# End of the expert stage: last product and scatter by column halves, y ahead of the splits, overflow branch turned round

## What is computed

```python
xn = rmsnorm(h, norm_ffn[1])
h = h + moe_swiglu(xn, router, w_gate, w_up, w_down)     # 8 experts, top 2 of 8 for each token
gate = jax.nn.sigmoid(rmsnorm(h, ple_norm[1]) @ ple_gate[1])
h = h + gate * (p[1] @ ple_proj[1])                      # the "embedding" step
```

## Time and profile before

| | us |
|---|---|
| median of 3 runs | 2064.74 |
| lowest, highest | 2061.09, 2072.94 |
| the profiled execution, its own time | 2058.84 |
| its span from the first to the last instruction | 2057.0 |
| experts end, last product | 1521.06 |
| first gate product (0,0) starts | 1548.00 |

### The profile page before, as it was taken

How to read it: one execution, slowest core, us unless ns; L and a number is a source line. 1 busy time by engine, 2 the same in 40 slices (tenths; PEclk the granted TensorE clock), 3 DMA queues, 4 the chain that set the end, 5 groups by cost and what they waited for, 6 DMA issues and landing times.

```text
span 2057.0 us, 27400 instructions
## 1 busy us (share of the span) xinstructions
PE 1990.2 (97%) x10513; PEld 1680.8 (82%) x10513; DVE 1541.8 (75%) x1513; ACT 1243.8 (60%) x1346; POOL 0.2 (0%) x4
## 2 busy tenths in 40 slices
PE   8999999999899999999999999999979999999998
PEld 7879998887788888888888888888857787878786
DVE  4575556556788988988898898988877756766575
ACT  4554445555677777777777777776757444344532
POOL 0000000000000000000000000000000000000000
PEclk9999999999999999999999999999989999999999
DMA  8617555423799999999999999999974541344320
GB/s 262 215 41 254 187 188 165 155 82 121 254 376 345 357 370 338 374 334 367 341 354 379 326 374 346 358 376 326 375 270 130 179 144 62 123 164 164 123 82 21
DMA packets 243012, 504.08 MB, mean 245 GB/s; under 512 B 12136, under 2 KB 58984, under 8 KB 242920
## 3 DMA queue, kind: packets, MB, share of 16 engines
q1 hardware_dynamic: 242632, 502.71, 68.8%
q10 hardware_dynamic: 288, 0.11, 0.0%
HBM read 501.73 MB, written 1.05 MB: 244 GB/s over the span
## 4 chain that ended last, share of the span: by engine, by line
PE 84%; DVE 8%; ACT 4%; issue 2%; DMA 1%; SPq 1%; DVEq 0%; ACTq 0%
PE bank L693 25%; PE bank L695 25%; PE bank L694 25%; DVE low L1748 2%; PE bank L779 2%; PE bank L1123 1%; PE bank L1080 1%; PE bank L805 1%; ACT high L1299 1%; PE bank L664 1%; ACT high L1501 1%; PE bank L1208 1%; PE bank L796 1%; DMA raw<-in_w_in 1%; DVE y_lo L2361 1%
## 5 line engine op out<-in xcount | busy, mean ns | idle before, releaser
L2318 DVE TENSOR_TENSOR low<-raw,high 128x2048 fp32r<-128x2048 f32 x336 | 768.2, 2290 | 105.4 <-ACT high L1501 104.0
L1501 ACT ACTIVATE high<-raw 128x2048 fp32r<-128x2048 f32 x336 | 644.8, 1920 | 247.5 <-PE bank L695 246.2
L1748 DVE TENSOR_TENSOR low<-raw,high 128x2048 fp32r<-128x2048 f32 (+1 forms) x138 | 310.2, 2259 | 160.4 <-ACT high L1299 159.9
L1299 ACT ACTIVATE high<-raw 128x2048 fp32r<-128x2048 f32 (+1 forms) x138 | 260.7, 1894 | 165.0 <-PE bank L695 155.3
L693 PE MATMUL bank<-high,xg_hi 128*128 128x512 f32 x896 | 353.6, 395 | 2.2 <-DVE xg_lo L2301 2.2
L695 PE MATMUL bank<-high,xg_lo 128*128 128x512 f32 x896 | 349.4, 390 | 0.0
L694 PE MATMUL bank<-low,xg_hi 128*128 128x512 f32 x896 | 348.8, 389 | 0.0
L693 PE MATMUL bank<-high,xT_hi 128*128 128x512 f32 (+1 forms) x576 | 226.7, 394 | 4.1 <-DVE xT_lo L1764 1.8
L695 PE MATMUL bank<-high,xT_lo 128*128 128x512 f32 (+1 forms) x576 | 221.4, 384 | 0.0
L694 PE MATMUL bank<-low,xT_hi 128*128 128x512 f32 (+1 forms) x576 | 221.0, 384 | 0.0
L693 PE MATMUL bank<-high,hT_hi 128*128 128x512 f32 x536 | 210.1, 392 | 0.0
(11 more groups left out here) (315 smaller groups left out, 2366.1 us busy)
## 6 DMA issues: line engine op xcount, KB each, us to landing
raw<-in_moe_w_gate SPq DMA_DIRECT2D x112, 1024.0 KB, 5.5
raw<-in_moe_w_up SPq DMA_DIRECT2D x112, 1024.0 KB, 5.6
raw<-in_moe_w_down SPq DMA_DIRECT2D x112, 1024.0 KB, 5.7
raw<-in_w_in SPq DMA_DIRECT2D x63, 1024.0 KB, 5.4
raw<-in_w_out SPq DMA_DIRECT2D x20, 1024.0 KB, 4.9
raw<-in_dense_w_gate SPq DMA_DIRECT2D x11, 1024.0 KB, 5.3
raw<-in_dense_w_up SPq DMA_DIRECT2D x11, 1024.0 KB, 5.4
raw<-in_dense_w_down SPq DMA_DIRECT2D x11, 1024.0 KB, 5.0
```

The source lines that it names most:

```text
L1299: act.activation(high[:, slot, 0:k * n], raw[:, raw_slot[piece], 0:k * n], ACT.Copy).then_inc(high_done, 1)
L1501: act.activation(high[:, k % PARTS, :], raw[:, slot, :], ACT.Copy).then_inc(s["high"], 1)
L1748: dve.tensor_tensor(low[:, slot, 0:k * n], src, high[:, slot, 0:k * n].bitcast(F32), ALU.subtract).then_inc(low_done, 1)
L2318: dve.tensor_tensor(low[:, k % PARTS, :], raw[:, at0 + k % slots, :], high[:, k % PARTS, :].bitcast(F32), ALU.subtract).then_inc(s["low"], 1)
```

## The change

On all three engines the end of the last expert moves out of `expert` and `scatter` into a `finish`, and the beginning of the embedding step (`embedding_in`) moves into the branch. In the order of the code:

- **Down product.** The last half of the last expert's last down product runs column half 0 (bank 4) first, then column half 1; after the first a new semaphore `half` rises. The number of matmuls is the same.
- **y by halves.** ACT makes `y_hi` of half 0 behind `half`, that of half 1 behind the whole product. DVE raises `ylow` after each half. PE's scatter and DVE's adds go by columns first (n: token tile n % 2, columns n // 2).
- **Splits.** In the last expert only pp is split ahead (AHEAD = 1). pg0 half 0 is split behind y, at the start of `embedding_in(1)` (ACT: between y and the squares; DVE: between the last add and the norm); pg0 half 1 after the branch, by `splits(pp)`.
- **Branch.** `If(over < 1)` with the usual arm first: `finish` and `embedding_in(1)`, then `Else` with `finish`, the second pass, `finish` and `embedding_in(1)` again. The branch stands ahead of `finish`. PE reads the flag behind expert 0.
- **What is inside the usual arm.** PE: scatter, projection, transposes, gate product (0,0). ACT: root table, y, split of pg0 half 0, squares, root, the four takes of the projection, `xT_hi`. DVE: y, adds, split of pg0 half 0, 1/rms, rows, `xT_lo`.

```diff
+AHEAD = 1
@@ PE: product, in the last expert
-                            for f in range(2):
+                            columns_first = is_last and (j, half) == (GROUPS - 1, 1)
+                            for n in range(4):
+                                f, c = (n % 2, n // 2) if columns_first else (n // 2, n % 2)
...
+                                if columns_first and n == 1:
+                                    last.then_inc(s["half"], 1)
@@ PE
                 product("down", GROUPS - 1)
-                if is_last:
-                    scatter(e + 1, s, 12, turn_bank, range(4))
+            def finish(s):
+                for n in range(4):
+                    t, c = n % 2, n // 2
+                    cols = slice(c * CHUNK, (c + 1) * CHUNK)
+                    pe.wait_ge(s["ylow"], N_EXPERTS + c)
+                    pe.wait_ge(s["tfree"], 14 * N_EXPERTS - 5 + n)
+                    b = bank[6 + n % 2]
+                    pe.matmul(b[:, :], pickT[:, tok(t)], y_hi[:, cols], start=True, stop=False)
+                    pe.matmul(b[:, :], pickT[:, tok(t)], y_lo[:, cols], start=False, stop=True).then_inc(s["tfull"], 1)
@@ PE: all_experts
                 expert(0, s, first, True, False)
+                over = None
+                if not again:
+                    pe.wait_ge(route_ready, 1)
+                    over = pe.value_load(flag_i[0:1, 0:1], min_val=0, max_val=1)
                 with pe.Fori(1, N_EXPERTS - 1) as e:
@@ PE: experts
-                all_experts(moe_sems[0], moe_first, False)
-                pe.wait_ge(route_ready, 1)
-                over = pe.value_load(flag_i[0:1, 0:1], min_val=0, max_val=1)
-                with pe.If(over > 0):
+                over = all_experts(moe_sems[0], moe_first, False)
+                with pe.If(over < 1):
+                    finish(moe_sems[0])
+                    embedding_in(1)
+                with pe.Else():
+                    finish(moe_sems[0])
                     pe.wait_ge(moe_sems[0]["tfree"], 14 * N_EXPERTS)
                     pe.nop().then_inc(moe_sems[1]["used"], RAW)
                     all_experts(moe_sems[1], RAW, True)
-                    pe.wait_ge(redo_low, PARTS)
+                    finish(moe_sems[1])
+                    pe.wait_ge(redo_low, AHEAD)
+                    embedding_in(1)
@@ PE: embedding_in ends with
                 norm(("ple", l))
+                rows_half([("gate", l, 0, t) for t in range(NT)], ("pg", l, 0), 0, name=("ple", l))
@@ ACT: expert
-                    elif not again:
+                    elif not again and q + PARTS < PER_EXPERT + AHEAD:
                         split(moe_first + N_EXPERTS * PER_EXPERT + q + PARTS - PER_EXPERT)
...
+            def finish(s, first):
+                for c, (done, count) in enumerate(((s["half"], 1), (s["used"], first + PER_EXPERT * N_EXPERTS))):
+                    act.wait_ge(done, count)
+                    act.activation(y_hi[:, c * CHUNK:(c + 1) * CHUNK], bank[4 + c][:, :], ACT.Copy,
+                                   scale=slot_gate[:, 0:1]).then_inc(s["y"], 1)
+            def embedding_in(l, table=True):
+                if table:
+                    sqrt_ahead()
+                else:
+                    split_next()
+                half_squares(("ple", l), 0)
+                half_squares(("ple", l), 1)
+                serve_rstd()
+                for j in range(2):
+                    for t in range(NT):
+                        take(("pproj", l, j, t), projected(j, t))
+                norm_high(("ple", l))
@@ ACT: behind the experts
-                    with act.If(over > 0):
+                    with act.If(over < 1):
+                        sqrt_ahead()
+                        finish(moe_sems[0], moe_first)
+                        embedding_in(1, False)
...
+                    with act.Else():
+                        finish(moe_sems[0], moe_first)
...
@@ DVE: expert as ACT's, and
+            def finish(s):
+                for c in range(2):
+                    y_low(s, N_EXPERTS - 1, c).then_inc(s["ylow"], 1)
+                for n in range(4):
+                    t, c = n % 2, n // 2
                     cols = slice(c * CHUNK, (c + 1) * CHUNK)
+                    dve.wait_ge(s["tfull"], 14 * N_EXPERTS - 3 + n)
+                    dve.tensor_tensor(h[:, t, cols], h[:, t, cols], bank[6 + n % 2][:, :],
+                                      ALU.add).then_inc(s["tfree"], 1)
+            def embedding_in(l):
+                if l == 1:
+                    dve.wait_ge(moe_sems[0]["tfree"], 14 * N_EXPERTS)
+                    mark().then_inc(h_ready, 1)
+                    split_next()
+                norm_rows(("ple", l))
+                norm_low(("ple", l))
@@ DVE: experts
-                with dve.If(over > 0):
+                with dve.If(over < 1):
+                    finish(moe_sems[0])
+                    embedding_in(1)
...
+                with dve.Else():
+                    finish(moe_sems[0])
```

More of the change, by code:

```diff
@@ L263, in program @@
         members_ready, rank_max, route_ready = sem("members_ready"), sem("rank_max_ready"), sem("route_ready")
-        moe_names = ("sel", "tfull", "thigh", "tfree", "silu", "hm", "y", "ylow", "step")
+        moe_names = ("sel", "tfull", "thigh", "tfree", "silu", "hm", "half", "y", "ylow", "step")
         moe_sems = [{n: sem(f"moe{p}_{n}") for n in moe_names} for p in range(2)]
@@ L1192, in layer_embedding, with embedding_out @@
                 norm(("ple", l))
+                rows_half([("gate", l, 0, t) for t in range(NT)], ("pg", l, 0), 0, name=("ple", l))
+            def embedding_out(l):
                 for j in range(2):
                     for half in range(2):
-                        rows_half([("gate", l, j, t) for t in range(NT)], ("pg", l, j), half,
-                                  name=("ple", l) if j == 0 else None)
+                        if (j, half) != (0, 0):
+                            rows_half([("gate", l, j, t) for t in range(NT)], ("pg", l, j), half,
+                                      name=("ple", l) if j == 0 else None)
                         if (l, j, half) == (0, 1, 0):
@@ L1305, in splits, with split_next @@
                     split_no[0] += 1
+            def split_next():
+                split(split_no[0])
+                split_no[0] += 1
             def high_rows_of(key, dst, scales=None):
@@ L1642, in _ @@
                         act.wait_ge(moe_sems[1]["tfree"], 14 * N_EXPERTS)
-                    split_no[0] = moe_first + N_EXPERTS * PER_EXPERT + PARTS
-                norm_sums(("ple", l))
-                for j in range(2):
-                    for t in range(NT):
-                        take(("pproj", l, j, t), projected(j, t))
-                norm_high(("ple", l))
+                        sqrt_ahead()
+                        embedding_in(1, False)
+                if l == 0:
+                    embedding_in(0)
                 splits(pieces_of["pp", l][0])
@@ L2357, in expert, with y_low, embedding_in @@
                         gathered(s, 9 * e + 8, (7, 6))
+                if is_last:
+                    return
                 for c in range(2):
-                    cols = slice(c * CHUNK, (c + 1) * CHUNK)
-                    dve.wait_ge(s["y"], 2 * e + c + 1)
-                    last = dve.scalar_tensor_tensor(out=y_lo[:, cols], in0=bank[4 + c][:, :], scalar=slot_gate[:, 0:1],
-                                                    in1=y_hi[:, cols].bitcast(F32), op0=ALU.mult, op1=ALU.subtract)
-                last.then_inc(s["ylow"], 1)
-                if is_last:
-                    scattered(s, e, 12, range(4))
+                    last = y_low(s, e, c)
+                last.then_inc(s["ylow"], 1)
+            def y_low(s, e, c):
+                cols = slice(c * CHUNK, (c + 1) * CHUNK)
+                dve.wait_ge(s["y"], 2 * e + c + 1)
+                return dve.scalar_tensor_tensor(out=y_lo[:, cols], in0=bank[4 + c][:, :], scalar=slot_gate[:, 0:1],
+                                                in1=y_hi[:, cols].bitcast(F32), op0=ALU.mult, op1=ALU.subtract)
+            def finish(s):
[3 more added lines that the diff above has]
+                    t, c = n % 2, n // 2
+                    cols = slice(c * CHUNK, (c + 1) * CHUNK)
+                    dve.wait_ge(s["tfull"], 14 * N_EXPERTS - 3 + n)
+                    dve.tensor_tensor(h[:, t, cols], h[:, t, cols], bank[6 + n % 2][:, :],
+                                      ALU.add).then_inc(s["tfree"], 1)
+            def embedding_in(l):
+                if l == 1:
[4 more added lines that the diff above has]
+                norm_low(("ple", l))
             def all_experts(s, first, first_slot, again):
@@ L2388, in experts @@
                     all_experts(moe_sems[1], RAW, P, True)
-                    for k in range(PARTS):
+                    finish(moe_sems[1])
+                    for k in range(AHEAD):
```

(3 more changed lines are left out.)

44 lines of the change are left out of this document (25 added, 19 removed).

## The result

The changed kernel takes 2053.11 us, the median of 14 runs (2046.09 to 2058.34); the kernel before, beside it, 2062.01 (14 runs). The ratio is 0.9945, with a 95% interval of 0.9933 to 0.9956: 11.3 us less, 9.1 to 13.8 (the medians differ by 8.9). The forecast was 2055.0, 9.7 us less, which lies inside that interval. The profiled execution took 2050.85 us; the forecast for it was 2049.1.

A forecast was written before the change was run, and what follows sets the result against it. TensorE, busy 97% of the span, was taken as the bound, so only its waits between experts and gate products counted. Gain 11.4 us at (0,1) less 1.7 for half clock, 9.7 off 2064.74: 2055.0 us, range 2047 to 2062.

The forecast's parts named there:

- Part 1: Behind the last product: y by halves starts scatter at 1521.3 and has `h` whole 6.3 us earlier.
- Part 2: Branch ahead of `finish`, not taken: costs nothing, with PE's flag read hidden; at most 1 us without that cover.
- Rival 4: Branch at the experts' end stalls PE 6.6 us although not taken; gain 6.4 us, 2058.3; chance 0.06.
- Part 3: Up to gate product (0,0): first gate matmul at 1532.6 in place of 1548.00, a gain of 15.4 us so far.
- Part 4: Jump ending the usual arm delays pg0 half 1's split: gain at (0,1) 11.4 us, less 1.7 for half clock.
- rival 1: Jumps at the usual arm's end cost 3.0 us, PE's 3.9, no clock loss; gain 14.3 us, 2050.4; chance 0.24.
- rival 2: Jumps at the usual arm's end take some 0.1 us; gain 15.4 us, 2049.3; chance 0.03.
- rival 3: Arm-end jumps take twice 5.7 us; gain 2.4 us, 2062.3; chance 0.18 including what lies between it and the forecast.
- Rival 5: PE's shifted loop body is fetched again each lap, costing 20.4 us; 2075.4, slower than before; chance 0.04.

The follow-up runs named there:

- e9: e5 with pg0 half 0 split ahead of y again (two splits ahead in place of one); 2054.2 us, measured one time.
- e5: Changed kernel with everything behind the branch written inside both arms, so the usual case jumps only at the program's end; 2044.99 us, ratio 0.9926.
- e10: e5 with the last half product in its old order, so both halves of y wait for its end; 2042.62 us, measured one time.
- e1: Changed kernel with y, scatter and splits (three ahead) as before, leaving the branch turned round alone; 2056.01 us, ratio 0.997.
- e2: Changed kernel with the branch back behind the scatter and taken, leaving y by halves and ahead of the splits alone; 2056.27 us, ratio 0.9965.
- e3: Changed kernel with the loads behind pg1 half 0 held until gate product (0,0) is done; 2048.62 us, ratio 0.9931.
- e8: The changed kernel measured again, unaltered, beside e4, e5 and e7; 2052.5 us, ratio 0.9953.
- e6: Changed kernel with the second pass left out of the other arm on PE, ACT and DVE; 2047.44 us, ratio 0.992.
- e4: Changed kernel with pg0 half 1 split as the last work inside the usual arm of ACT and DVE; 2054.27 us, ratio 0.9949.
- e7: Changed kernel with e4 and e3 together: pg0 half 1 split inside the arm and loads held; 2049.5 us, ratio 0.9936.

## Why the prediction was right

**Part 1, y and scatter: right.** The scatter starts at 0.21 us behind the last product and the last add ends at 1526.9, 4.28 behind it; the prediction had 0.24 and 4.24. Before it took 5.71 us to the scatter, with three pieces split ahead. e9 has 2.34 with two, and e5 0.21 with one; with one and the old column order it is 1.56 (e10).

**Part 2, the branch not taken: right.** It takes 71 ns, and no gap but the 0.21 us stands ahead of the scatter. PE's read hides as costed: its sequencer spends 0.9 us on it from 653.7 on, and PE has no wait between 650 and 660. Rival 4 (6.6 us there) falls. The Trainium skill, "Advanced Engine Details and Errata", Control Flow Timing, gives 108 ns for compare and branch: of the branch that isn't taken it is of the right size, of the one over a long arm it is fifty-seven times under (6142 ns).

**Part 3, up to (0,0): right.** Predicted 11.5 us behind the last product, measured 11.43; predicted gain 15.4, measured 26.94 - 11.43 = 15.5. The projection ran at full clock (e1's and e2's did not, behind waits of 5.7 and 6.95 us). `yf` ends at 1531.25, 0.2 us before the transposes start at 1531.47: the projection and the rows arrive together, as the working had it.

**Part 4, what is late next: right.** ACT's sequencer passes its last wait 10.8 us behind the last product and ACT goes on at 16.57: 5.8 us, where I took 5.7 from DVE's gap at the same load (390 GB/s then, 392 now). The other value that I weighed, 3.0 us for ACT's jump in the kernel before, I had read at 122 GB/s; that stretch ran 1.2 us past the jump, and during the jump itself the DMA was nearly quiet, with 26 GB/s:

```profile
1521.28:1524.24 2.96, 0.00 (x0) 0.00 (x0) 2.54 (x2) 2.94 (x4) 0.00 (x0) 1.00 0.20 26
```

So that row was of the kind of e3's, and not of a medium load. (0,1) predicted at 21.0 behind the last product, measured at 20.86. PE's idle time ahead of it was predicted at 4.0 and measured at 3.74; the half clock behind it was charged with 1.7, and from (0,1) to (1,0) it took 8.88 us where it took 7.11 before, 1.8 more. Sum: 9.7 predicted at the end of the gates, 9.9 measured. That the two agree to 0.2 us is partly luck: the same kernel in e8 lost 1.0 us more to the clock and has 8.9. That the jump and not the split is what is late was only argued then; e3, e5 and e6 show it, each by another way, and e4 shows that PE's own jump stands right behind ACT's.

**The rivals.** Cheap jumps (rival 1) is what e3 did by a quiet DMA: 3.3 us for PE's jump, no loss of clock at (0,1), and the gates end 13.7 us earlier than before where the rival had 14.3. Free jumps (rival 2) is e6, and e5 in effect: their (0,1) is 15.5 us earlier than before, where the rival had 15.4. The changed kernel is neither. Dear jumps (rival 3) fell: none took more than 6.2 us in it. Rival 5, a loop body that has to be fetched again, fell by the queues of the changed kernel from 790 to 1400, where the packets of data are the only ones, as in the earlier trace rows:

```profile
q1 hardware_dynamic: 91414, 216.13, 97.1%
```

**What was off.** The profiled execution took 2050.85 us and not 2049.1. The step that is missing isn't one of the change: in the stretch 480.0 to 483.4 the clock was at 0.50, which put the last product 1.56 us later. e5, whose code up to there is the same, has it at 1521.06 again, exactly as before. The terms that the expectations of the experiments had wrong by over a microsecond hold a half clock each: how long it lasts (e1), whether it comes behind a wait of about 2 us (e4, e9, and e3's and e7's rest). e10's, without one, was 12.2 for (0,0) and the trace has 12.36.

**Open.** Upstream of the last product, one stretch of 6.8 us at half clock near 522 is in the kernel before, in the changed kernel and in e5 alike. In which executions others are added to it (3.4 us in the changed kernel's profile, 20 us in e6's, none in e5's), and why the one behind the same wait doesn't come at all or lasts 3.4 or 6.8 us, was not settled. Nor do the runs show from what length on an arm is a long one: the jumps here lead over some tens or hundreds of instructions (e6) or over the whole second pass. The stretches at half clock are what separates the lowest from the highest run of one kernel: over a whole execution the mean granted clock was 0.994 in the changed kernel's lowest run (2046.09 us) and 0.988 in its highest (2058.34), and 0.006 of 2050 us is 12.3 us, as much as the two runs differ by.

## What to carry to other kernels

Put the usual case first behind a branch, and then ask what stands behind the jump that ends it: the fetch of a far target isn't gone but moved, and it costs nothing only where an engine has nothing to deliver behind it (the program's end, e5) or where its sequencer is further ahead than the fetch lasts (PE in e1 and e7). A producer that feeds the bound engine must not have its next piece right behind such a jump. Where a result that others wait for shares an engine with preparatory work, look at the order on that engine first, then at making the result in smaller portions: here one split moved behind y was worth some 1.7 us (an estimate, see e9), or 2.9 with the clock that the longer wait cost, and the column order 0.9.

## What the hardware showed that was not expected

- The price of PE's jump over the long arm follows the load of the DMA while it lasts: 6142 ns at 337 GB/s (changed), 3462 at 91 (e1), 3322 at 10 (e3), 3802 at 9 (e7), 3843 at 4 (e5). Over a short arm it is 313 ns at 389 GB/s (e6).
- A wait of 2.09 us (e4) and one of 2.34 us (e9) were each followed by a stretch at 0.50 of the clock, while one of 1.48 us (e3) was not. The same wait of 2.21 us was followed by such a stretch in six traces and by full clock in the other six. Between two executions of the same code with the same wait (3.74 and 3.69 us) the stretch lasted 3.4 us in one and 6.7 us in the other.
- Under a high load the jump isn't one number, and it doesn't follow the GB/s alone: 6142 ns (337 GB/s, changed), 6142 (358, e4), 6591 (391), 7470 (350, e2).
